# Seven half-size products for a pair of tiles, with weight sums made by accumulating loads, in a two-block transformer kernel

## What is computed

```python
f = rmsnorm(h, norm_ffn_g[i])
h = h + (jax.nn.silu(f @ w_gate[i]) * (f @ w_up[i])) @ w_down[i]
...
out = rmsnorm(h, norm_final_g)
return out[:, N_META:]
```

## Time and profile before

| | |
|---|---|
| median of 3 runs | 2308.55 us (2307.75 to 2308.59) |
| profiled execution, its own time | 2309.27 us |
| its span, first to last instruction | 2307.3 us |
| granted TensorE clock, mean | 0.999 |
| busy share PE / PEld / DVE / ACT / POOL | 99% / 88% / 56% / 39% / 1% |
| DMA | 197.47 MB, mean 86 GB/s |
| chain that ended last | PE 93%, DVE 3%, ACT 2% |

### The profile page before, as it was taken

One profiled execution on the slowest core, in us unless ns is written; L12 is line 12 of the kernel. 1 busy time (PEld: TensorE's weight loads), 2 busy tenths in 40 slices (PEclk: granted clock), 3 DMA queues, 4 the chain that ended last, 5 costly groups with the idle time before them and its releaser, 6 DMA issues.

```text
span 2307.3 us, 36725 instructions
## 1 busy us (share of the span) xinstructions
PE 2287.0 (99%) x15423; PEld 2038.2 (88%) x15423; DVE 1285.3 (56%) x2258; ACT 909.8 (39%) x1566; POOL 34.5 (1%) x75
## 2 busy tenths in 40 slices
PE   9999999999999999999999999999999999999998
PEld 7798999999997898999899788978898888888887
DVE  5356576446643465766366566869455455443443
ACT  5356544224333465543144443223244444221232
POOL 2000000000000000000000000000000000000001
PEclk9999999999999999999999999999999999999999
DMA  4221223222312221323223222223222232332331
GB/s 137 92 72 47 86 83 100 87 80 92 110 58 74 93 61 43 102 92 107 77 92 109 80 75 74 91 85 98 92 65 65 65 101 92 100 110 74 100 109 55
DMA packets 57910, 197.47 MB, mean 86 GB/s; under 512 B 8545, under 2 KB 12547, under 8 KB 57747
## 3 DMA queue, kind: packets, MB, share of 16 engines
q1 hardware_dynamic: 55827, 189.73, 25.6%
q0 software_dynamic: 1344, 4.36, 0.6%
q10 hardware_dynamic: 576, 1.05, 0.1%
HBM read 192.98 MB, written 2.13 MB: 85 GB/s over the span
## 4 chain that ended last, share of the span: by engine, by line
PE 93%; DVE 3%; ACT 2%; issue 1%; DMA 0%; POOL 0%; SPq 0%; ACTq 0%; DVEq 0%; POOLq 0%
PE G L1079 76%; PE G L1153 7%; PE X L1365 1%; PE X L1320 1%; PE X L1447 1%; PE X L1343 1%; DVE wL L1950 1%; PE X L1431 1%; PE X L1148 1%; ACT wH L1489 1%; PE X L1416 1%; PE X L1079 1%; PE X L1403 0%; PE X L1279 0%; PE X L1375 0%
## 5 line engine op out<-in xcount | busy, mean ns | idle before, releaser
L1079 PE MATMUL G<-aH,wH 128*128 128x264 f32 (+2 forms) x2992 | 759.0, 316 | 4.0 <-DVE wL L1950 3.6
L1079 PE MATMUL G<-aL,wH 128*128 128x264 f32 (+2 forms) x2992 | 738.1, 309 | 0.0
L1079 PE MATMUL G<-aH,wL 128*128 128x264 f32 (+2 forms) x2992 | 737.5, 309 | 0.0
L1489 ACT ACTIVATE wH<-raw 128x512 fp32r<-128x512 f32 (+3 forms) x477 | 386.9, 829 | 666.6 <-PE G L1079 612.1
L1950 DVE TENSOR_TENSOR wL<-raw,wH 128x512 fp32r<-128x512 f32 (+3 forms) x477 | 443.7, 941 | 207.1 <-ACT wH L1489 205.1
L1079 PEld LDWEIGHTS G<-aH,wH 128*128 128x128 f32 x2992 | 488.0, 189 | 43.5 <-issue 9.9
L1079 PEld LDWEIGHTS G<-aH,wL 128*128 128x128 f32 x2992 | 485.6, 188 | 29.4
L1079 PEld LDWEIGHTS G<-aL,wH 128*128 128x128 f32 x2992 | 486.2, 188 | 26.9 <-issue 0.2
L2102 DVE TENSOR_TENSOR hT<-G,hT 128x528 f32<-128x528 f32 (+1 forms) x83 | 58.1, 700 | 215.8 <-PE G L1079 215.8
L1079 PE MATMUL G<-hidH,wH 128*128 128x264 f32 (+1 forms) x528 | 140.7, 321 | 1.4 <-DVE hidL L2186 1.4
L1079 PE MATMUL G<-hidL,wH 128*128 128x264 f32 (+1 forms) x528 | 141.1, 322 | 0.0
(11 more groups left out here) (348 smaller groups left out, 2689.9 us busy)
## 6 DMA issues: line engine op xcount, KB each, us to landing
raw<-weights SPq DMA_DIRECT2D x276, 512.0 KB, 3.5
raw<-weights SPq DMA_DIRECT2D x48, 704.0 KB, 4.0
raw<-weights SPq DMA_DIRECT2D x12, 384.0 KB, 3.1
negc<-sums POOLq DMA_DIRECT2D x16, 264.0 KB, 4.4
out_t<-hT SPq DMA_DIRECT2D x16, 128.0 KB, 1.8
raw<-weights SPq DMA_DIRECT2D x14, 128.0 KB, 2.1
hT<-x_t ACTq DMA_DIRECT2D x4, 256.0 KB, 4.8
hT<-x_t SPq DMA_DIRECT2D x4, 256.0 KB, 7.0
```

Of the source, the lines that this page charges most:

```text
L1079: done = e.matmul(m.pair(i)[0:M, bank, 0:n], a[:, k, 0:M], b[:, kx, lo - t0:lo - t0 + n], start=(k == 0 and c == 0), stop=(k == nk - 1 and ...
L1489: e.activation(m.high(i)[:, c], m.raw[:, r, c], ACT.Copy).then_inc(s.w_hi, 1)
```

## The change

In 19 of the 22 pairs of the last feed-forward (hidden tiles 3 to 10 of half one, all 11 of half two) the two tiles `u2` and `g2` are replaced by seven blocks, called here by their number p. The pair is a 2x2 block product: the weights' blocks are up and gate by lower and upper half of the 8 sub-blocks, the operand's are lower and upper half of the sub-blocks by first and second 256 positions. Strassen's method makes the four results of seven products instead of eight.

- **Weights.** Blocks 1 (up, lower), 2 (up, upper) and 3 (gate, upper) are plain loads of 128 x 512. Blocks 5, 6 and 4 are made in the `raw` place of block 1, one after the other, each by a DMA that adds (`accum_op`): 5 = 1 + gate lower, 6 = 5 + gate upper, 4 = 6 + up upper. Block 7 is a plain load and one added. POOL issues the adding DMAs, in its part of the step `split`, once DVE has split what the place held. There are 76 of them.
- **Rings.** The ring of split weights has five places of 512 columns. The `raw` buffers are eleven places of 512 columns, three of them for the chain 1, 5, 6, 4 (pairs in turn).
- **Order.** `by_seven()` sets it. From the third pair on the products stand as 6 of one pair, 1 of the next, 7 of the first, 2 and 5 of the next, 3 and 4 of the first. Each block's split stands four products ahead of its product.
- **Operand.** It must be normalised before its sums are made: `norm7` (8 of 128x512), four sums of 128x1024 (`sum7`), and the split of seven operands of 128x1024 each (`high7` on ACT, `low7` on DVE). Blocks 1, 2, 5 and 6's operands go to a new buffer `seven`, those of 7, 4 and 3 over `aH` and `aL`, after the last plain tile.
- **PE.** A product (`prod7`) is 4 sub-blocks x 3 matmuls of 256 columns. Products 6, 7, 3 and 4 go on adding in the PSUM bank in which 1 or 5 stood, after ACT (`p1st`, `u2nd`, `p5th`) or DVE (`c22`) has read it.
- **Out of PSUM.** ACT copies 1, 5, 6 and 4's results, DVE adds 2, 7 and 3's, all 128x256. Evacuation by `rbc` is gone.

The core of the diff:

```diff
+SEVEN = {2: 3}
+XSLOT, YSLOT, ZSLOT, WSLOT = (0, 1, 2), (3, 4), (5, 6, 7), (8, 9, 10)
...
+def by_seven(first):
+    out, pairs = [], list(range(first, 11))
+    if pairs:
+        out += [(pairs[0], 1), (pairs[0], 2), (pairs[0], 5)]
+    for n, jj in enumerate(pairs):
+        if n + 2 < len(pairs):
+            nx = pairs[n + 1]
+            out += [(jj, 6), (nx, 1), (jj, 7), (nx, 2), (nx, 5), (jj, 3), (jj, 4)]
...
     for half in range(2):
-        for jj in range(11):
-            fm(("u2", half, jj), "w_up_2", 0, 128 * (11 * half + jj))
-            fm(("g2", half, jj), "w_gate_2", 0, 128 * (11 * half + jj))
+        gated(2, half, ("w_up_2", 0, 0), ("w_gate_2", 0, 0), ("u2",), ((), (), ("g2",)))
...
+    def seven():
...
+            while state["split"] < len(PLAN) and WAS.get(state["split"], -1) < i and ROLE[state["split"]][0] != "out":
+                step("split", state["split"], 0, 1)
+                state["split"] += 1
+            if pieces:
+                step(*pieces.popleft())
+            step("prod7", f, half, jj, p)
+            step({1: "p1st", 2: "c11", 5: "p5th", 6: "u2nd", 7: "c22", 3: "c12", 4: "c21"}[p], f, half, jj)
...
+                pieces.extend(("%s7" % what, f, half, jj) for what in ("silu", "gate", "hidh", "hidl"))
...
+        if p == 1:
...
+            if paired[g]:
+                e.wait_ge(s.sums_dve, SUMS_DVE[("c12",) + paired[g]])
+                e.wait_ge(s.sums_act, SUMS_ACT[("c21",) + paired[g]])
+            paired[g] = key
+        elif p == 6:
+            e.wait_ge(s.sums_act, SUMS_ACT[("p1st",) + key])
+        elif p == 7:
+            e.wait_ge(s.sums_act, SUMS_ACT[("u2nd",) + key])
...
+        for k in range(4):
+            for c, (a, b) in enumerate(((wh, xh), (wh, xl), (wl, xh))):
+                done = e.matmul(out, a[:, k, :], b[:, k, :], start=(p in (1, 2, 5) and k == 0 and c == 0),
+                                stop=(k == 3 and c == 2), skip_group_check=p not in (1, 2, 5))
...
+        for c in ADD_AT.get(i, ()):
+            block = c
+            if c in SECOND:
+                block, first, times = SECOND[c]
+                e.wait_ge(s.ring[first], 16 * times)
+            else:
+                e.wait_ge(s.w_lo, SPLIT_DONE[RAWWAS[c]][-1])
+            e.dma_start(m.raw(c), weights(W, block), accum_op=ALU.add).then_inc(s.ring[RING[c]], 16)
```

More of the change, by code:

```diff
@@ L168, in places @@
 def places():
-    place, was, n, last = {}, {}, 0, {}
+    place, was, n = {}, {}, 0
+    last, k = [-1] * (NW * WMAX), 0
     for i, role in enumerate(ROLE):
@@ L610, in fg @@
             for half in range(2):
-                for jj in range(11):
+                made = operands(2) if 2 in SEVEN and not half else []
+                for jj in range(11 if 2 not in SEVEN else SEVEN[2] * (1 - half)):
                     first = half + jj == 0
-                    yield from fm(hold=first)
-                    yield from fm(hook=("rms", ("ffn2",)) if first else None)
+                    now, made = ([], made) if first else (made[:16], made[16:])
+                    yield from fm(hold=first, before=dict(enumerate(now[0:8])))
+                    yield from fm(hook=("rms", ("ffn2",)) if first else None, before=dict(enumerate(now[8:16])))
+                assert not made
+                if 2 in SEVEN:
+                    if not half:
+                        flush()
+                        last_operands(2)
+                    yield from seven()
                 for _ in range(8 - half):
@@ L737, in banks @@
     for i, role in enumerate(ROLE):
+        if role[0] == "seven":
+            first = AT[role[:4] + (1,)]
+            if i == first:
+                out[i], g = g, 1 - g
+            else:
+                out[i] = out[first]
+            continue
         if role[0] == "gq" and role[2] == 1:
@@ L799, in new @@
             return ctx.enter_context(nc.semaphore(name))
-        self.ring = [new(f"ring{i}") for i in range(NR)]
+        self.ring = [new(f"ring{i}") for i in range(NR + 12)]
         self.vecs = new("vecs")
@@ new lines, in silu7, with hidh7 @@
+    def silu7(f, half, jj):
+        table["set"] = "other"
+        if f == 2:
+            e.wait_ge(s.sums_dve, SUMS_DVE["c12", f, half, jj])
+            e.activation(m.Gt[:, jj % 2, :], m.Gt[:, jj % 2, :], ACT.Silu, scale=-1.0).then_inc(s.gate, 1)
+            return
+        n = nth7(f, half, jj)
+        av = m.Av[:, 2 * (jj % 2) + 1, NM if f else 0:L]
+        e.wait_ge(s.taps, 2 * n + 1)
+        e.activation(av, av, ACT.Silu).then_inc(s.gate, 1)
+    def hidh7(f, half, jj):
+        high, low, product = hid_tile(m, f, jj)
+        if half and jj == 0:
+            e.wait_ge(s.chunk, AT[("d2", 0, 7) if f == 2 else ("down", f, 0, 7)] + 1)
+        e.wait_ge(s.gated, nth7(f, half, jj) + 1)
+        e.activation(high, product, ACT.Copy).then_inc(s.hid_hi, 1)
@@ new lines, in low7, with c11 @@
+    def low7(f, p):
+        high, low = m.seven_operand(f, p)
+        e.wait_ge(s.seven_hi, NTH["high7", f, p])
+        e.tensor_tensor(low, m.seven_source(f, p), high.bitcast(F32), ALU.subtract).then_inc(s.seven_lo, 1)
+    def c11(f, half, jj):
+        i, n = AT["seven", f, half, jj, 2], STAGE[f][1]
+        out = m.pair_out(f, jj, 0)[:, 0:n]
+        e.wait_ge(s.sums_act, SUMS_ACT["p1st", f, half, jj])
+        e.wait_ge(s.chunk, i + 1)
+        e.tensor_tensor(out, out, X[:, 2 + BANK[i], 0:n], ALU.add).then_inc(s.sums_dve, 1)
@@ new lines, in gate7, with hidl7 @@
+    def gate7(f, half, jj):
+        n, product = nth7(f, half, jj), hid_tile(m, f, jj)[2]
+        u = m.U[:, jj % 2, :] if f == 2 else m.Av[:, 2 * (jj % 2), NM if f else 0:L]
+        e.wait_ge(s.gate, n + 1)
+        if f == 2:
+            e.wait_ge(s.sums_act, SUMS_ACT["c21", f, half, jj])
+        else:
+            e.wait_ge(s.taps, 2 * n + 2)
+        e.tensor_tensor(product, product, u, ALU.mult).then_inc(s.gated, 1)
+    def hidl7(f, half, jj):
+        high, low, product = hid_tile(m, f, jj)
+        e.wait_ge(s.hid_hi, nth7(f, half, jj) + 1)
+        e.tensor_tensor(low, product, high.bitcast(F32), ALU.subtract).then_inc(s.hid_lo, 1)
```

351 lines of the change are left out of this document (301 added, 50 removed).

## The result

The changed kernel took **2410.16 us** (median of 4 runs, 2408.09 to 2412.96), and the kernel before took 2308.57 in the same rounds: ratio 1.044, 95% interval 1.042 to 1.046. That is 101.6 us slower where +36 was forecast, above the range's 2395.

The account below looks back on a forecast made before the run. PE bound the kernel, busy 99%. Seven products could save 19.8 us, but the preparation's 14.6 us and the chain of adding loads at L = 3.6 made it +36 us: 2309.3 to 2345, range 2300 to 2395.

Parts of the forecast that it names:

- PE alone: PE's time per pair: seven products take 10.08 us instead of 11.12, at most 19.8 us less over 19 pairs.
- The preparation: Operand's norms, sums and low parts on DVE during pairs 1 and 2, 19.5 us into 11.9 free; PE loses 14.6 us.
- The chain: Adding loads for blocks 5 and 6, each awaiting the last: period 4.7 + 2L, 11.9 us a pair against PE's 10.08.
- L: Time from POOL's issue of an adding load to its landing, taken as 3.6 us; forecast case 3.0 to 4.4.
- the prediction's own sums: Both halves' seven-product stretches, computed from L: together a change of -97.3 + 37L, +36 us at L = 3.6.
- the end of a half: After the last pair's blocks 5 and 6 are split, five products remain before the first d2 tile: 7.2 us.
- the load reads its destination besides: An adding load's extra read in the last feed-forward's rounds; priced only in rival 3, 3.1 MB a round, 9.8 of 10.08 us.
- rival 3: Adding loads choke the DMA engines in the rounds: L 4.5 to 5.2, +69 to +95 us, 2378 to 2404; chance 0.12.
- The warning of the Trainium skill: DVE in a 2-port mode may delay POOL's DMA issue; counted no more than the trace's 538 to 587 ns an issue.

Follow-up runs that it names:

- late operands: Against the run with plain SP loads and no sums: operands of products 7, 4 and 3 split behind the first three products; 2302.77 us, 0.9966 of the kernel before.

## Why the prediction had the direction and not the size

- **PE alone: right.** 10.08 us for seven products; 9.98 measured where nothing else bound. The gain was there, and 7 us of it survived the preparation in the version without sums and with late operands.
- **The preparation: right, 2 us too long.** The second product, forecast at 1979.6, started at 1978.22 in a trace that stands about 0.6 us later than that of before at `hid2L`: PE lost 12.6 us and not 14.6. DVE's rows came in the order laid out; the high part that DVE has to wait for was counted.
- **The chain: right in its links and its constant.** 4.7 us were forecast between landings. In the steady rounds it is 4.95, in the first ones of each half less, and over the nine periods of half two what is left beside the landings is 4.7 each.
- **The step that failed is the size of L**: "The nearest row is two plain 264 KB together on POOL's queue, 3.6 us ... I take L = 3.6". A plain 256 KB on this queue landed in 2.9 us (2.8 to 3.1 in the stretch shown, issues back to back included). So the plain load was put 0.7 us too high, and what adding costs, 2 us in the median, was put at nothing. The adding load took 4.1 us or a little more with none ahead of it, and 6.2 as block 5's, where it followed another and ran beside SP's. On the chain that ended last, half one's 15 landings sum to 77.5 us and half two's 22 to 117.3, where a load issued behind another counts from the first issue of the two: L = 5.2 and 5.3. By the prediction's own sums that is 23.5 and 38.1 us over L = 3.6, 62 of the 66 us missed.
- **A second term was short: the end of a half, put at five products, 7.2 us.** Block 4's sum "has seven products' time and doesn't bind", said the prediction. For a half's last pair it hasn't: product 4 stands four products behind product 6 there and not six, and block 4's sum is the chain's next link. From the low part of block 6 to the first `d2` tile is 2100.47 - 2088.98 = 11.5 us in half one and 2339.19 - 2328.87 = 10.3 in half two, 7.4 us more together. In half one PE's granted clock of 0.72 in the last three products is a part of it (36 matmuls in 6.08 us, at full clock 4.3):

```profile
2088.98 0.28 issue
2089.26 4.15 DMA raw<-weights
2093.41 0.02 issue
2093.43 0.63 ACT wH L1747
2094.06 0.28 ACT G L2013
2094.35 0.04 issue
2094.39 6.08 PE G L1338 x36
```

With these landings, this end, and the chain's start in half one 2.2 us earlier than laid out, the prediction's sums give 136.5 and 177.5 us; 136.3 and 177.4 were measured.

- **What "the load reads its destination besides" costs was named and not priced.** It was in rival 3 alone, with 0.12. That rival had nearly the right L (4.5 to 5.2) and its end of 2404 is 6 us short. Its mechanism, queueing on full engines, is right in part: adds hold the DMA engines 1.8 times as long a MB as plain loads. But in the changed kernel those engines were busy 59% and 62% (windows above), and the greater part of L is what an adding load takes with none ahead of it. Queueing is the rest (the runs with an earlier block 5 and, besides, with small plain loads: 17 and 30 us less than the changed kernel).
- **The warning of the Trainium skill, page "SBUF — State Buffer" (Who interferes with whom), that DVE can keep GpSimd from writing descriptors** was weighed and left out of the sum. The runs bear that out: POOL's issues of adding loads took 867 ns in the median and 851 at the least, and each of the longer ones (1.14 to 1.57 us, 20 of 76) began before the issue ahead of it on POOL had ended; plain ones took 536 to 538. The prediction took the adding load's issue for a plain one's, 0.33 us short, and no run shows a wait for DVE on top. The warning is for DVE's 2-port mode, and the same section of the Trainium skill says that `tensor_tensor` has no 2-port mode; every DVE instruction in the rounds of the changed kernel is of that kind.
- **The range** ended at L = 5, just under what the unpriced operation then took. Its upper bound should have come from the longest landing in the rows, 6.5 us, and reached +143.

## What to carry to other kernels

Count what a new operation does between its issue and its landing before taking a plain one's time for it, and where no row shows it, let the range reach to the multiple that the work suggests. When a schedule is written for the middle of a loop, follow its chain to the last round too: a value with time to spare there can be the next link at the end. Where a value is made in steps, each of which must land before the next is issued, the period is the number of steps times the whole latency, whatever the bandwidth; here only the two sums with slack in their round could go by DMA at no loss. Fewer products on a full PE are worth just what the pitch says (1.1 us of 11.1 a pair here), and every pass that feeds them competes for an engine that was half idle only in the mean (here DVE).

## What the runs showed of the hardware

- An adding DMA of 128x512 floats on POOL's queue: 865 ns to issue (plain 536), 4.1 us to land with none ahead of it (plain 2.9), 5.1 in the mean beside SP's loads and 6.2 behind another besides; 2.4 us with 64 columns. It holds the 16 DMA engines 6.4 us a MB, plain ones 3.5.
- GpSimd's addition of 128x512 took 1518 ns in the mean with DVE at work, and DVE's split of the same size 1006 rather than 691 ns.
- Matmuls of 256 columns ran 9.98 us for 84, 0.119 each. Right after a wait of 2.8 us, 512-column ones went at 0.42 us (1963.69, 1964.11, 1964.54 in the changed kernel), against 0.2317; the granted clock was 0.50 from 1963.2 to 1965.8, the 1.2 GHz level, and 1.00 from 1966 to 1970.
